# Reading out the GLA sample states with the queries stationary

## The reference, cut to what matters

```python
b = jnp.cumsum(gb, axis=2)                       # log decay, over the 4 tokens
att = jnp.einsum('bhtk,bhsk,bhtsk->bhts', qb, kb, decay)
o = (jnp.einsum('bhts,bhsv->bhtv', att, vb)      # inside the 4 tokens
     + jnp.einsum('bhtk,bhkv->bhtv', qb * jnp.exp(b), S))   # the read-out of the state S
S_new = exp(b_last) * S + jnp.einsum('bhsk,bhsv->bhkv', kb * jnp.exp(b_last - b), vb)
```

## Time and profile before

| what | us |
|---|---|
| median of 3 runs | 3434.81 |
| lowest and highest run | 3433.54, 3440.26 |
| span of the profiled execution, first to last instruction | 3423.6 |
| PE busy in the span | 3257.8 (95%) |
| DVE, ACT, POOL busy | 1738.4, 1299.5, 297.2 |

### The profile page before, as it was taken

How to read it: one execution, slowest core, us unless ns; L and a number is a source line. 1 busy time by engine, 2 the same in 40 slices (tenths; PEclk the granted TensorE clock), 3 DMA queues, 4 the chain that set the end, 5 groups by cost and what they waited for, 6 DMA issues and landing times.

```text
span 3423.6 us, 65170 instructions
## 1 busy us (share of the span) xinstructions
PE 3257.8 (95%) x25412; PEld 2999.5 (88%) x25412; DVE 1738.4 (51%) x2375; ACT 1299.5 (38%) x1678; POOL 297.2 (9%) x306
## 2 busy tenths in 40 slices
PE   5899999998899999999999799999889999999998
PEld 2599989988788988988889699999879999999997
DVE  1466666665543443434444556556455444454444
ACT  0444444443433332333332444344244333343333
POOL 0011111111300000000001211011021000000001
PEclk7899999999999999999999899999899999999998
DMA  8967777773488688687787455654435555555552
GB/s 330 339 215 233 228 227 237 232 222 116 128 269 266 193 265 268 198 267 245 215 264 236 136 154 180 206 184 144 154 120 167 166 157 165 159 166 163 158 166 71
DMA packets 536811, 685.47 MB, mean 200 GB/s; under 512 B 21409, under 2 KB 468441, under 8 KB 536281
## 3 DMA queue, kind: packets, MB, share of 16 engines
q1 hardware_dynamic: 481090, 626.15, 58.1%
q10 hardware_dynamic: 55488, 55.91, 5.2%
HBM read 651.30 MB, written 30.67 MB: 199 GB/s over the span
## 4 chain that ended last, share of the span: by engine, by line
PE 88%; DVE 4%; ACT 3%; DMA 3%; issue 2%; SPq 0%; POOL 0%; ACTq 0%; DVEq 0%; POOLq 0%
PE main L462 25%; PE main L463 24%; PE main L464 24%; PE bank L472 5%; DMA raw<-in_w_ada 2%; PE bank L559 2%; PE bank L830 2%; PE bank L754 1%; PE bank L599 1%; ACT w_hi L933 1%; DVE z L1614 1%; DMA raw<-in_hg_w_in 1%; PE bank L836 1%; DVE a_lo L1335 1%; ACT ln_h L947 0%
## 5 line engine op out<-in xcount | busy, mean ns | idle before, releaser
L1330 DVE TENSOR_TENSOR w_lo<-raw,w_hi 128x1024 fp32r<-128x1024 f32 x804 | 987.7, 1230 | 1391.7 <-ACT w_hi L933 1387.8
L933 ACT ACTIVATE w_hi<-raw 128x1024 fp32r<-128x1024 f32 x804 | 850.7, 1059 | 1743.1 <-PE main L464 1676.5
L462 PE MATMUL main<-a_hi,w_hi 128*128 128x288 f32 x4368 | 1344.1, 308 | 62.0 <-DVE a_lo L1335 43.1
L463 PE MATMUL main<-a_lo,w_hi 128*128 128x288 f32 x4368 | 1305.1, 299 | 0.0
L464 PE MATMUL main<-a_hi,w_lo 128*128 128x288 f32 x4368 | 1304.5, 299 | 0.0
L462 PEld LDWEIGHTS main<-a_hi,w_hi 128*128 128x128 f32 x4368 | 837.1, 192 | 144.1 <-issue 110.0
L463 PEld LDWEIGHTS main<-a_lo,w_hi 128*128 128x128 f32 x4368 | 838.2, 192 | 4.1 <-issue 1.7
L464 PEld LDWEIGHTS main<-a_hi,w_lo 128*128 128x128 f32 x4368 | 836.7, 192 | 0.0
L462 PE MATMUL main<-act_hi,w_hi 128*128 128x288 f32 x2048 | 613.0, 299 | 0.0
L463 PE MATMUL main<-act_lo,w_hi 128*128 128x288 f32 x2048 | 605.0, 295 | 0.0
L464 PE MATMUL main<-act_hi,w_lo 128*128 128x288 f32 x2048 | 604.8, 295 | 0.0
(11 more groups left out here) (251 smaller groups left out, 2065.9 us busy)
## 6 DMA issues: line engine op xcount, KB each, us to landing
raw<-in_w_ada SPq DMA_DIRECT2D x384, 512.0 KB, 4.2
raw<-in_w_up SPq DMA_DIRECT2D x256, 512.0 KB, 3.9
raw<-in_w_down SPq DMA_DIRECT2D x256, 512.0 KB, 3.8
raw<-in_hg_w_in SPq DMA_DIRECT2D x128, 512.0 KB, 6.2
raw<-in_gla_w_in SPq DMA_DIRECT2D x100, 512.0 KB, 3.8
raw<-in_hg_w_out SPq DMA_DIRECT2D x32, 512.0 KB, 3.5
gl_s<-in_state_gla ACTq DMA_DIRECT2D x32, 512.0 KB, 4.7
out_new_gla_sample<-gl_s ACTq DMA_DIRECT2D x32, 512.0 KB, 3.5
```

Of the source, the lines that this page charges most:

```text
L462: mm(out, hi, x_hi[:, kb, :], start=kb == 0, stop=False)
L463: mm(out, hi, x_lo[:, kb, :], start=False, stop=False)
L933: F(w_hi[:, st.split_slot(g)].rearrange("p k n -> p (k n)"), raw[:, slot, :], ACT.Copy).then_inc(hi_ready, 1)
L1330: V.tensor_tensor(w_lo[:, s].rearrange("p k n -> p (k n)"), raw[:, slot, :], w_hi[:, s].rearrange("p k n -> p (k n)").bitcast(F32), ALU.su ...
```

## The change

The read-out swaps its operands. The queries become stationary and the state moves. `gl_read_out(n, q)` handles two sequences (2q and 2q+1) at once, with four f32 matmuls: for each of the two sequences and each of the two key halves j, 32 columns of queries are held in one column tile (a strip of 32 columns) of the array, and the state's 512 columns stream through; the four results go to four groups of 32 partitions of bank b7, and the four calls (q = 0 to 3) add up there. It is called at step 23 (q = 0) and at steps 1, 3 and 5 of the next head, ahead of that step's `gl_sample`. So that the 32 columns hold only the right sequence's 4 queries and zeros elsewhere, DVE writes the decayed queries into `suf`, cleared first, in groups of 4 at a stride of 36 (`gl_key_mul`, in the place of `key_mul` for GLA). At step 5 ACT copies b7 (tokens on partitions, 512 values) to `gl_os`, which lies in `v`. At step 6 `gl_sample_out` puts the inside term (the former `gl_intra`) into b6 and adds four products with `gl_os` as the stationary operand and a 0/1 selection matrix `sel` (32 columns) as the moving one: they add the two key halves and turn the result back to values on partitions. `gl_sample` keeps only the update L836. The prompt's output blocks swap b6 and b7. DVE builds `sel` once, ahead of the stage, and waits for `or_done` ahead of the clearing of `suf` at step 6.

```diff
--- before.py
+++ after.py
@@ -227,7 +227,13 @@
                      [("gl.sp", [P, GLA_V]), ("gl.low", [P, T])] + common("gl") + [
         ("gl.v", [P, 4, T]), ("gl.g", [P, 4, T]), ("gl.att", [P, 3, P]), ("gl.atts", [64, TS]),
         ("gl.vt", [P, 2, GLA_V]), ("gl.kt", [P, 2, 2, P]), ("gl.vs", [96, GLA_V], F32R), ("gl.ks", [96, 2, P], F32R),
-        ("gl.ksm", [96, 2, 2, P], F32R), ("gl.s0", [P, 4, 2, GLA_V]), ("gl.s1", [P, 2, 2, GLA_V]), ("gl.gk2", [P, 2, P])])
+        ("gl.ksm", [96, 2, 2, P], F32R), ("gl.s0", [P, 4, 2, GLA_V]), ("gl.s1", [P, 2, 2, GLA_V]), ("gl.gk2", [P, 2, P]), ("gl.sel", [P, NB // 2, 2, TB])])
+    gl_qz = gl["suf"][:, :, :].rearrange("p j t -> p (j t)").rearrange("p (j b q c) -> p j b q c", j=2, b=2, c=36)
+    gl_qw = gl["suf"][:, :, :].rearrange("p j t -> p (j t)").rearrange("p (j b c) -> p j b c", j=2, b=2)
+    gl_os = gl["v"][:, :, :].rearrange("p v t -> p (v t)")[:, 0:GLA_V]
     yout = mem.scratch([(act0, act1)], [("yout.y", [P, 3, D])])["y"]
     main = nc.alloc_psum_tensor("main", [P, 4, 512], F32)
@@ -274,7 +280,7 @@
         names = ("gate_log gate_lin gate_mix gate_soft gates_ready k_ready silu_soft silu_lin silu_exp exp_ready sums_ready "
                  "level_ready level_done level_read kd_exp kd_ready turned turned_read s_turned "
                  "s_turned_read s_split s_masked o_done o_read oi_done oi_read squared summed rstd_ready o_ready "
-                 "att_set ps_done ps_read ps_stored ss_done ss_read gk_done gk_read gk2_loaded gk2_set").split()
+                 "att_set ps_done ps_read ps_stored ss_done ss_read or_done or_read qz_set sel_set gk_done gk_read gk2_loaded gk2_set").split()
         return {name: S(f"{m}_{name}") for name in names} | {
             "s0_loaded": [S(f"{m}_s0_loaded{i}") for i in range(loads)],
             "s_stored": [S(f"{m}_s_stored{i}") for i in range(stores)]}
@@ -807,38 +813,54 @@
                 last = mm(b6[:, :], gl["kt"][:, t, j, :], gl["vt"][:, t, :], start=t == 0, stop=t == 1)
             last.then_inc(G["ps_done"], 1)
-        def gl_intra(n):
-            pe.wait_ge(G["s_split"], 2 * n + 2)
-            pe.wait_ge(G["level_read"], 9 * n + 3)
-            for v in range(4):
-                mm(b7[:, 32 * v:32 * v + 32], gl["vs"][0:64, v * P:(v + 1) * P].bitcast(F32), gl["atts"][:, :], start=v == 0,
-                   stop=False, skip_group_check=True)
+        def gl_read_out(n, q):
+            for b in (2 * q, 2 * q + 1):
+                pe.wait_ge(G["s0_loaded"][b % 4], 32 * n + 16 * (b // 4 + 1))
+            if q == 0:
+                pe.wait_ge(G["kd_ready"], n + 1)
+                pe.wait_ge(G["s_split"], 2 * n + 2)
+            for b in range(2):
+                for j in range(2):
+                    g = 32 * (2 * b + j)
+                    last = mm(b7[g:g + 32, :], gl_qw[:, j, b, 32 * q:32 * q + 32],
+                              gl["s0"][:, (2 * q + b) % 4, j, :], start=q == 0, stop=q == 3, skip_group_check=True,
+                              tile_position=(0, g))
+            if q == 3:
+                last.then_inc(G["or_done"], 1)
         def gl_sample(n, b):
-            slot = b % 4
-            pe.wait_ge(G["s0_loaded"][slot], 32 * n + 16 * (b // 4 + 1))
             pe.wait_ge(G["s_masked"], 8 * n + b + 1)
             if b == 0:
                 pe.wait_ge(G["level_read"], 9 * n + 9)
                 pe.wait_ge(G["turned_read"], 3 * n + 3)
             else:
                 pe.wait_ge(G["ss_read"], 8 * n + b)
-            for v in range(4):
-                for j in range(2):
-                    last = mm(b7[:, 32 * v + TB * b:32 * v + TB * (b + 1)], gl["s0"][:, slot, j, v * P:(v + 1) * P],
-                              gl["qd"][:, j, TB * b:TB * (b + 1)], start=False, stop=j == 1 and b == NB - 1,
-                              skip_group_check=True)
-            if b == NB - 1:
-                last.then_inc(G["oi_done"], 1)
             for j, bank in enumerate((b4, b5)):
                 last = mm(bank[:, :], gl["ksm"][:, b % 2, j, :], gl["vs"][:, :], start=True, stop=True)
             last.then_inc(G["ss_done"], 1)
+        def gl_sample_out(n):
+            pe.wait_ge(G["s_split"], 2 * n + 2)
+            pe.wait_ge(G["level_read"], 9 * n + 3)
+            for v in range(4):
+                mm(b6[:, 32 * v:32 * v + 32], gl["vs"][0:64, v * P:(v + 1) * P].bitcast(F32), gl["atts"][:, :], start=v == 0,
+                   stop=False, skip_group_check=True)
+            pe.wait_ge(G["or_read"], n + 1)
+            pe.wait_ge(G["sel_set"], 1)
+            for v in range(4):
+                last = mm(b6[:, 32 * v:32 * v + 32], gl_os[:, v * P:(v + 1) * P],
+                          gl["sel"][:, :, :, :].rearrange("p q b t -> p (q b t)"), start=False, stop=v == 3,
+                          skip_group_check=True)
+            last.then_inc(G["oi_done"], 1)
         def gl_out_block(n, v):
-            bank = (b6, b7)[v % 2]
+            bank = (b7, b6)[v % 2]
             if v == 1:
                 pe.wait_ge(G["oi_read"], n + 1)
             if v >= 2:
@@ -858,6 +880,8 @@
         def gl_step(n, s, own, prev):
             pn = n - 1
             if prev:
+                if s in (1, 3, 5):
+                    gl_read_out(pn, (s + 1) // 2)
                 if s <= 6:
                     gl_sample(pn, s + 1)
                 if s == 0:
@@ -865,6 +889,7 @@
                 if s == 6:
                     pe.wait_ge(*((G["gk_read"], 2 * n + 2) if own else (G["ps_read"], 2 * pn + 2)))
+                    gl_sample_out(pn)
                 if 6 <= s <= 9:
                     gl_out_block(pn, s - 6)
                 if s == 10:
@@ -886,7 +911,7 @@
                 elif s == 22:
                     gl_prompt_state(n, 0)
                 elif s == 23:
-                    gl_intra(n)
+                    gl_read_out(n, 0)
                     gl_sample(n, 0)
         for s in range(4):
@@ -1210,14 +1235,17 @@
                     gl_store(pn, s)
                     if s < 4 or own:
                         gl_load(*((pn, s + 4) if s < 4 else (n, s - 4)))
+                if s == 5:
+                    act.wait_ge(G["or_done"], pn + 1)
+                    F(gl_os, b7[:, :], ACT.Copy).then_inc(G["or_read"], 1)
                 if s == 6:
                     act.wait_ge(G["oi_done"], pn + 1)
-                    F(o_buf[:, cols(4 * pn, 4), TP:T], b7[:, 0:128].rearrange("p (v t) -> p v t", v=4), ACT.Copy
+                    F(o_buf[:, cols(4 * pn, 4), TP:T], b6[:, 0:128].rearrange("p (v t) -> p v t", v=4), ACT.Copy
                       ).then_inc(G["oi_read"], 1)
                 for v, at in enumerate((6, 7, 8, 9)):
                     if s == at:
                         act.wait_ge(G["o_done"], 4 * pn + v + 1)
-                        F(o_buf[:, cols(4 * pn + v, 1), 0:TP].rearrange("p a t -> p (a t)"), (b6, b7)[v % 2][:, 0:TP],
+                        F(o_buf[:, cols(4 * pn + v, 1), 0:TP].rearrange("p a t -> p (a t)"), (b7, b6)[v % 2][:, 0:TP],
                           ACT.Copy).then_inc(G["o_read"], 1)
                 if s == 9:
                     act.wait_ge(G["att_set"], 1)
@@ -1472,6 +1500,17 @@
             V.tensor_tensor(buf["qd"][:, :, :], buf["qd"][:, :, :], buf["q"][:, :, TP:T], ALU.mult
                             ).then_inc(M["kd_ready"], 1)
+        def gl_key_mul(n):
+            dve.wait_ge(G["kd_exp"], n + 1)
+            V.memset(gl["suf"][:, :, :], 0.0).then_inc(G["qz_set"], 1)
+            V.tensor_tensor(gl["x"][:, 1], gl["x"][:, 1], gl["k"][:, :, :], ALU.mult)
+            dve.wait_ge(G["qz_set"], n + 1)
+            for j in range(2):
+                last = V.tensor_tensor(gl_qz[:, j, :, :, 0:TB],
+                                       gl["qd"][:, j, :].rearrange("p (q b t) -> p b q t", b=2, t=TB),
+                                       gl["q"][:, j, TP:T].rearrange("p (q b t) -> p b q t", b=2, t=TB), ALU.mult)
+            last.then_inc(G["kd_ready"], 1)
         def hg_step(n, s, own, prev):
             pn = n - 1
             if prev:
@@ -1724,13 +1763,15 @@
                     dve.wait_ge(G["gate_log"], n + 1)
                     step(V.scalar_tensor_tensor(out=pre, in0=t1, scalar=0.0, in1=t2, op0=ALU.min, op1=ALU.subtract))
                     step(V.tensor_scalar(pre, pre, 1.0 / GATE_NORM, None, ALU.mult))
+                    if prev:
+                        dve.wait_ge(G["or_done"], n)
                     V.memset(gl["suf"][:, :, :], 0.0).then_inc(G["gates_ready"], 1)
                 if 11 <= s <= 18:
                     level_mul(G, gl, n, s - 10)
                 if 11 <= s <= 19:
                     gl_read(n, s - 11, prev)
                 if s == 19:
-                    key_mul(G, gl, n)
+                    gl_key_mul(n)
                 elif s == 20:
                     silu_lin(G, 2 * n + 1, gl["g"][:, 0:2, :], panel(GLA, 4))
                 elif s == 21:
@@ -1757,6 +1798,11 @@
```

(5 more changed lines are left out.)

## The result

| | median us | lowest, highest | runs |
|---|---|---|---|
| before, beside the runs of after | 3434.28 | 3433.54, 3440.26 | 4 |
| after | 3383.86 | 3381.17, 3387.45 | 4 |

The ratio is 0.9851, with an interval from 0.9838 to 0.9865: 1.5% faster, by 50.4 us (the first experiment shows that about 8 us of it belong to which runs of the kernel before stood beside it). I had said 3395 us and a range that began at 3386. The profiled execution of after took 3381.17 us and its span is 3379.3.

What follows compares the result with a forecast made beforehand. PE was taken to bound the GLA heads. Gains of 26.2 us on PE before the last head's tile 23 ends, 5.6 for the clock and 8 in the tail sum to 39.8, so 3434.8 becomes 3395 us, range 3386 to 3412.

Steps and rivals of the forecast that it cites:

- the base of the sum: Whole run: span 3423.6 us plus 11.2 us around it, kept unchanged, from which the gain was subtracted.
- Read-out groups: Heads, steps 23, 1, 3, 5: four column tiles run side by side, 1.15 us a group, bounds 0.85 to 1.54.
- Selection and inside term: Step 6: selection's 8 instructions cost 0.9 us a head; inside term L815, 1.01 us, only moves there from step 23.
- The clock at step 23: Behind step 23 in 4 heads: without thin work the full clock returns, products 0.13 us apart, 5.6 us gained.
- the clock falls at step 6: Rival, step 6: 1.4 us come back in three heads and some in the tail, 3400 us; chance 0.12.
- Up to R: Until the end of the last head's tile 23 (R): 26.2 us less on PE, plus 5.6 us for the clock.
- The state traffic: Rival, steps 0 to 6: state transfers need 340 GB/s, may top at 328 or stay at 282; 3398 to 3415; chance 0.18.
- any wait for `gl_s0` inside the heads: Failure sign: PE showing waits for `gl_s0` (state loads) inside the heads would mean the prediction fails.
- The tail: From the last head's tile 23 end to first output block: sample 2 still 10.7 us in; gain 8 us (5 to 12.5).
- the column tiles would not run side by side: Rival, read-out groups: 3.4 us a group with 512 columns, tail gives 5 us, 3431 us, no change; chance 0.04.
- PE would stall for states: Rival, `gl_read_out` 2 and 3 in the heads: each read waits 7.8 us, slower from 15 us, 3442 us; chance 0.04.
- DVE's key work, or_done at step 6 and ACT's copy at step 5: Heads, steps 19, 6 and 5: added DVE and ACT work costed at nothing; the key work has 1.9 us of cover.

Runs made afterwards that it cites:

- the first experiment: The kernel before and the changed kernel each run again without edit: before 3427.56 us (ratio 1.000), changed 3384.67 us (ratio 0.9866).
- the experiment with full work: Kernel before, tail read-outs of samples 2 to 7 replaced (but for one product) by two unused full-array 512-column f32 products per update: 3431.23 us, ratio 0.9998.
- DVE's order: Changed kernel with DVE doing states 1, 2, 3, 5, 7 and their masks earlier in the GLA tail: 3385.03 us, ratio 0.9866.
- each group twice: Changed kernel with every read-out group issued twice, so the read-out counts double: 3395.86 us, ratio 0.99.
- the experiment on one tile: Changed kernel with all four read-out products of a group on the first column tile and the same 32 partitions of b7: 3420.20 us, ratio 0.997.

## Why the prediction was wrong at its edge and right in its mechanism

**The step that failed is the base of the sum.** I wrote that the 11.2 us between the span of 3423.6 and the median of 3434.8 lie "around it" and would stay. They were not around it: in every profiled run of this study that has both, time and span are 1.7 to 1.9 us apart. The other 9.3 us were a difference between two executions: the profiled one had a tail of 40.8 us, and the timed ones, which have no trace, took the time of those with a tail like the 49.3 us shown above. The difference of 8.5 us between these tails goes with the thin read-outs, so I carried over a cost that the change removes. With 1.9 us in the place of 11.2 the same sum gives 3385.7 us, 1.8 from what was measured. The clue was in the numbers that I had: I took 11.2 us on trust as overhead, where a run of 3440.26 beside two of 3434 should have made me ask whether the profile was of the same kind.

The 11.1 us of the miss (3395.0 - 3383.9) close: 9.3 from this step and 4.5 from the span (3383.8 forecast, 3379.3 found), less 2.7 by which the median run of after lies above the profiled one. The 4.5 are 3.5 ahead of the stage, 2.4 in the tail and -0.5 behind it, less 0.9 up to R. The 3.5 are luck: both programs are the same there, and in the second trace of after the stage begins 2.2 us later than in before.

**Read-out groups, 1.15 us forecast: right, a little high.** 0.99 us and 0.10 ahead of it were measured. Doubled, 0.87 is columns. I had scaled the part that isn't columns from the adaLN group, 0.34 us; here it is 0.22 with the part ahead. The estimate of 1.08 us, from what the Trainium skill's page "TensorE: Matmul & The Clock Gate", part 3, gives for three column tiles, comes nearer than my 1.15. Its share for four would be 3.17 times, an estimate, where this kernel shows 3.55 / 0.99 = 3.6. The drain at a change of tiling mode, which the Trainium skill's page "TensorEngine Tiling (Array Packing)", tiling modes, states, has no row of its own here; if it is there, it is within these 0.22 us.

**Selection and inside term: right.** 0.91 and 1.01 us, forecast 0.9 and 1.0.

**The clock at step 23: right.** The products behind it stand 0.13 us apart, and putting thin work back brings 0.24 and 4 to 5 us back beside its own time. The rival that the clock falls at step 6 is refuted: the products behind the selection stand 0.13 us apart, and 1.9 us of thin work in a row leaves the clock up.

**Up to R, 31.8 us forecast, 30.9 found.** With the measured terms it would have been 42.9 + 1.0 - 13 x 1.09 - 2.7 + 5.6 = 32.6. The difference to 30.9 is more than covered by PE's idle time: 1.1 to 1.4 us in two heads, just behind step 23, with no releaser in the profile (in both traces of after), and 0.5 us of a state load; before had 0.5 us of the first kind. The first kind is like the idle time met in the experiment with full work, and as open.

**The state traffic: the rival did not come, by little.** I had written that the stretch would ask for 340 GB/s and a share of 1.04, and that the transfers might top at 328. They gave 339 GB/s at a share of 0.97, in 31.60 us where I had worked out 32.0. The one price was 0.5 us, for a load that took 8.00 us to land. I had named any wait for `gl_s0` inside the heads as a sign that the prediction fails; this one came, and it was too small to carry anything. The tails of the experiments with DVE's order and with each group twice, where PE waits up to 1.23 and 2.02 us for a load, show that this cover is thin.

**The tail: right in kind, and of two sizes.** Sample 2 at R + 10.7 was right. Against the quicker group the tail gave 10.4 us where I said 8, with a granted clock of 0.94 and not near the lower level as I had assumed: a tile took 6.7 us, the lower end of my 6.4 to 8.2. Against the slower group it gave 49.3 - 30.4 = 19 us, above my upper end of 12.5. That is the same 9 us as in the failed step, seen from the tail.

**The other rivals.** That the column tiles would not run side by side is what the experiment on one tile looks like, and it is not what the change does. I had priced it at 3431 us; it came to 3420, as its tail takes 33.5 us and gives 7.2 us against the quicker group and 15.8 against the slower, where I had put 5. That PE would stall for states by 7.8 us a read is refuted by the 0.5 us above. DVE's key work, or_done at step 6 and ACT's copy at step 5 cost nothing: no wait for them is in the list of PE's waits.

## What to carry to other kernels

Before a sum is put on a median, compare the profiled execution with the timed ones: if they are further apart than the two or three microseconds that lie around a span, the profile may show another kind of execution than the median, and what tells the two kinds apart may be the very work that the change touches. An f32 matmul with few moving columns and a large stationary operand pays for the instruction and not for the columns; turning it so that the many columns move helps only together with column tiles, which here was 35 of the 43 us. Removing such thin work gives back its own time and, where it had left the clock at its lower level (behind 2.8 us of it at step 23 and in the tail, not behind 1.7 to 1.9 us in the heads), also that of the full-width work behind it.

## What the runs showed of the hardware that was not expected

- One program, two groups of times 10 us apart on one core (26 runs at 3423.8 to 3429.5 us, 15 at 3433.8 to 3440.0). In the one trace of each, they go with whether the granted clock comes back between the thin groups of the tail (1.84 us a group) or stays at 1.2 GHz (3.41 us). Where the thin read-outs of the tail are gone or replaced by full products, there is one group.
- Full work keeps the clock up also with waits between: 0.95 with PE busy 84% of 35.9 us, against 0.62 with PE busy 90% of 49.3 us when the work was thin. With neither in their place it was 0.83 (busy 72% of 29.9 us), and 0.94 (63% of 28.2 us) in the kernel without any read-out.
- Four column tiles with 512 columns each run 3.6 times as fast as on one tile, and entering and leaving costs some 0.2 us for each group.
- PE shows idle time of 1 to 2.5 us at single places, with no releaser in the trace, and the number of such places changes with edits far from them (2.1 us in the last 988 us of before, 14.3 us in the same work of the experiment with full products, which ran on another chip, and 5.8 us with thin work put back in the tail). The cause is open.
